# RWKV-7 recurrence slot: rank products, gates and decay sums one pair of heads ahead, head sums as 64-row products

## What is computed

```python
w_log = -softplus(-(w0 + tanh(xw @ w1) @ w2)) - 0.5
decay = exp(-exp(w_log))
a = sigmoid(a0 + (xa @ a1) @ a2)
kk = heads(k * k_k)
kk = kk / maximum(sqrt(sum(kk * kk, axis=-1)), 1e-12)
k = k * (1.0 + (a - 1.0) * k_a)
def step(S, inp):      # scan over the tokens, per head
    sa = einsum('bhvk,bhk->bhv', S, -kk_t)
    S = S * w_t + sa[..., None] * (kk_t * a_t) + v_t[..., None] * k_t
    return S, einsum('bhvk,bhk->bhv', S, r_t)
mean, var = y.mean(-1), y.var(-1)          # per head
y = (y - mean) * rsqrt(var + eps) * ln_w + ln_b
y = y + sum(rh * kh * r_k, axis=-1) * vh   # the bonus
out = (y * silu(z)) @ w_o
```

## Time and profile before

| | us |
|---|---|
| runs (3) | 2902.17, 2904.07, 2904.54 |
| median | 2904.07 |
| the profiled execution | 2901.24 |
| its span, first to last instruction | 2899.5 |
| PE busy | 2794.3 (96%) |
| DVE busy | 1337.7 (46%) |
| ACT busy | 1135.9 (39%) |

### The profile page before, as it was taken

How to read it: one execution, slowest core, us unless ns; L and a number is a source line. 1 busy time by engine, 2 the same in 40 slices (tenths; PEclk the granted TensorE clock), 3 DMA queues, 4 the chain that set the end, 5 groups by cost and what they waited for, 6 DMA issues and landing times.

```text
span 2899.5 us, 81414 instructions
## 1 busy us (share of the span) xinstructions
PE 2794.3 (96%) x37076; PEld 2632.0 (91%) x37076; DVE 1337.7 (46%) x2213; ACT 1135.9 (39%) x1559; POOL 108.1 (4%) x92
## 2 busy tenths in 40 slices
PE   6999999999999999999889899999999999999997
PEld 5899999999997888887789889999999999999997
DVE  7334313323327887787632364344443334444324
ACT  5344323324315555555432343343333343334322
POOL 0000000000001111111000000000000000000000
PEclk8999999999999999999999999999999999999999
DMA  3333333333311111112132242223222223222323
GB/s 124 110 104 110 111 111 111 112 111 141 104 67 47 53 53 53 53 53 78 31 130 88 81 143 75 96 75 98 89 89 75 97 75 97 90 89 75 125 89 108
DMA packets 79637, 262.25 MB, mean 90 GB/s; under 512 B 15936, under 2 KB 25920, under 8 KB 58816
## 3 DMA queue, kind: packets, MB, share of 16 engines
q1 hardware_dynamic: 70080, 239.23, 24.6%
q10 hardware_dynamic: 9216, 17.83, 1.6%
HBM read 216.06 MB, written 40.97 MB: 89 GB/s over the span
## 4 chain that ended last, share of the span: by engine, by line
PE 48%; ACT 1%; DVE 1%; issue 0%; DVEq 0%; ACTq 0%
PE t_pair L129 40%; PE t_lev L1596 1%; PE t_tok L1659 1%; PE t_pair L139 1%; PE t_lev L1670 1%; PE t_tok L1677 1%; PE t_tok L1637 0%; PE t_lev L1647 0%; PE t_tok L1552 0%; PE t_lev L1649 0%; PE t_lev L1609 0%; PE t_tok L1620 0%; PE t_tok L1629 0%; DVE keep_o L2179 0%; PE t_lev L1604 0%
## 5 line engine op out<-in xcount | busy, mean ns | idle before, releaser
L129 PE MATMUL t_pair<-t_x_hi,keep_w_hi 128*128 128x272 f32 x3008 | 660.1, 301 | 17.3 <-DVE t_x_lo L1992 9.1
L129 PE MATMUL t_pair<-t_x_lo,keep_w_hi 128*128 128x272 f32 x3008 | 623.8, 288 | 0.0
L129 PE MATMUL t_pair<-t_x_hi,keep_w_lo 128*128 128x272 f32 x3008 | 623.2, 288 | 0.0
L129 PEld LDWEIGHTS t_pair<-t_x_hi,keep_w_hi 128*128 128x128 f32 x3008 | 469.9, 189 | 48.5 <-issue 26.6
L129 PEld LDWEIGHTS t_pair<-t_x_lo,keep_w_hi 128*128 128x128 f32 x3008 | 475.6, 189 | 0.0
L129 PEld LDWEIGHTS t_pair<-t_x_hi,keep_w_lo 128*128 128x128 f32 x3008 | 472.4, 188 | 0.0
L129 PE MATMUL w_pair<-a_x_hi,keep_w_hi 128*128 128x272 f32 x2016 | 428.5, 294 | 19.4 <-DVE a_x_lo L1045 18.5
L129 PE MATMUL w_pair<-a_x_lo,keep_w_hi 128*128 128x272 f32 x2016 | 419.5, 289 | 0.0
L129 PE MATMUL w_pair<-a_x_hi,keep_w_lo 128*128 128x272 f32 x2016 | 417.4, 288 | 0.0
L1031 DVE TENSOR_TENSOR keep_w_lo<-keep_raw,keep_w_hi 128x2048 fp32r<-128x2048 f32 x63 | 144.4, 2293 | 469.7 <-ACT keep_w_hi L784 469.7
L129 PEld LDWEIGHTS w_pair<-a_x_hi,keep_w_hi 128*128 128x128 f32 x2016 | 320.3, 189 | 25.8 <-issue 20.7
(11 more groups left out here) (359 smaller groups left out, 3785.9 us busy)
## 6 DMA issues: line engine op xcount, KB each, us to landing
keep_raw<-in_w_in SPq DMA_DIRECT2D x64, 1024.0 KB, 4.9
keep_raw<-in_hgrn_in SPq DMA_DIRECT2D x64, 1024.0 KB, 4.9
keep_raw<-in_rwkv_wo SPq DMA_DIRECT2D x16, 1024.0 KB, 4.9
keep_raw<-in_hgrn_wo SPq DMA_DIRECT2D x16, 1024.0 KB, 4.9
t_Ss<-in_hgrn_s SPq DMA_DIRECT2D x16, 512.0 KB, 4.4
out_hgrn_s<-t_Sd SPq DMA_DIRECT2D x16, 512.0 KB, 6.7
scr_r<-a_stage ACTq DMA_DIRECT2D x16, 272.0 KB, 2.2
scr_k<-a_stage ACTq DMA_DIRECT2D x16, 272.0 KB, 2.1
```

Of the source, the lines that this page charges most:

```text
L129: mm = pe.matmul(out[:, a, 0:TH], w, x[:, kt, a * TH:(a + 1) * TH], start=(kt == 0 and n == 0), stop=(kt == KT - 1 and n == 2))
```

## The change

It rewrites the lists of PE, ACT and DVE for the slots; SyncE's and POOL's stay as they are.

- mean, variance, bonus (from pair 1) and square_sum (from pair 2) call by_heads: for each half of the columns two products of 64 rows, one per head, in place of one of 128 rows.
- rank_w(h) moves from behind level_yt(4) to ahead of level_x(3), and the rank_a of the pair ahead, h, from the start of the next slot to ahead of level_x(4). gate_w, gate_a, decay_sum and sum_before follow: they are made for h in slot i. Only decay_before(j) stays at the slot's start.
- g_and_value_y moves ahead of the third sample step. sample_states is cut in two: sample_values ahead of strict, the rest behind chain(i, 1).
- u_y is one group, all of chain(i, c) lie between levels 1 and 4, and variance moves from ahead of level_x(4) to behind inclusive, ahead of level_x(5).
- On DVE the three y steps come behind mask_x(j, 5), as the last of the slot.

```diff
@@ -415,6 +415,13 @@
                     mm = pe.matmul(q[:, a, 0:TH], lhsT, rhs[:, a * TH:(a + 1) * TH], start=True, stop=True)
                 return mm
 
+            def by_heads(lhsT, rhs):
+                for a in range(2):
+                    for hh in range(2):
+                        mm = pe.matmul(q[rows(hh), a, 0:TH], lhsT[rows(hh), rows(hh)],
+                                       rhs[rows(hh), a * TH:(a + 1) * TH], start=True, stop=True)
+                return mm
+
             def quarter(out, o_half, lhsT, rhs, i_half, start=True, stop=True):
                 return pe.matmul(out[rows(o_half)], lhsT[rows(i_half)], rhs[rows(i_half)], start=start, stop=stop,
                                  skip_group_check=not (start and stop))
@@ -444,8 +451,6 @@
             def rank_w(h):
                 pe.wait_ge(s.w2w_in, 16 * (h + 1))
                 pe.wait_ge(s.ssm, h + 1)
-                if h >= 2:
-                    pe.wait_ge(s.lnv, h - 1)
                 over_halves(w2[:, 0, :], lora[0]).then_inc(s.lora_w, 1)
 
             def rank_a(j):
@@ -457,12 +462,15 @@
                 pe.wait_ge(s.ksq, h + 1)
                 if h >= 1:
                     pe.wait_ge(s.bv, h)
-                over_halves(k.bones[:, :], ksq).then_inc(s.ss_mm, 1)
+                (by_heads if h >= 2 else over_halves)(k.bones, ksq).then_inc(s.ss_mm, 1)
 
             def bonus(j):
-                pe.wait_ge(s.sga, j + 1)
+                if j < 2:
+                    pe.wait_ge(s.sga, j + 1)
+                else:
+                    pe.wait_ge(s.lnv, j - 1)
                 pe.wait_ge(s.rk, j + 1)
-                over_halves(k.bones[:, :], rk).then_inc(s.bonus_mm, 1)
+                (by_heads if j >= 1 else over_halves)(k.bones, rk).then_inc(s.bonus_mm, 1)
 
             def strict(j):
                 a, b = at[j % 2], bt
@@ -539,10 +547,12 @@
                     pe.wait_ge(s.sU, 3 * i + n)
                 stacked(cut(m_ps, 0), cut(Ms, 0), Rs if n == 0 else Us[(n - 1) % 2]).then_inc(s.sMU_mm, 1)
 
-            def sample_states(i):
+            def sample_values(i):
                 pe.wait_ge(s.sU, 3 * i + 3)
                 pe.wait_ge(s.Vm, i + 1)
                 stacked(m_ps, cut(toks, 1), Vm[:, :, :].rearrange("p b v -> p (b v)"), True, False)
+
+            def sample_states(i):
                 pe.wait_ge(s.Um, i + 1)
                 stacked(m_ps, cut(toks, 0), Um[:, :, :].rearrange("p b v -> p (b v)"), False, True
                         ).then_inc(s.sd_mm, 1)
@@ -603,13 +613,13 @@
                 pe.wait_ge(s.y_ev, i + 1)
                 pe.wait_ge(s.sy, i + 1)
                 pe.wait_ge(s.bv, min(i + 2, KT))
-                pe.wait_ge(s.ssm, min(i + 3, KT))
-                over_halves(k.center[:, :], ybuf).then_inc(s.mean_mm, 1)
+                pe.wait_ge(s.sga, min(i + 3, KT))
+                by_heads(k.center, ybuf).then_inc(s.mean_mm, 1)
 
             def variance(i):
                 pe.wait_ge(s.ysq, i + 1)
                 pe.wait_ge(s.yc, i + 1)
-                over_halves(k.bones[:, :], ysq).then_inc(s.var_mm, 1)
+                by_heads(k.bones, ysq).then_inc(s.var_mm, 1)
 
             def first_pair(n, kt):
                 if (n, kt) == (51, 2):
@@ -691,74 +701,74 @@
             for i in range(KT):
                 j, h = i + 1, i + 2
                 back, front, ahead = i >= 0, 0 <= j < KT, h < KT
-                if front and i:
-                    rank_a(j)
                 if back:
                     sample_step(i, 0)
                     first_right(i)
                     sample_step(i, 1)
+                    g_and_value_y(i)
                     sample_step(i, 2)
-                    g_and_value_y(i)
                     u_and_value_state(i)
                 if front:
                     bonus(j)
                 if back:
                     rho_rest(i)
                     u_state(i)
+                    sample_values(i)
+                if front:
+                    strict(j)
+                if back:
+                    chain(i, 1)
                     sample_states(i)
-                    chain(i, 1)
-                if front:
-                    strict(j)
+                if front:
+                    level_x(j, 1)
                 if back:
                     chain(i, 2)
                 if ahead:
                     square_sum(h)
+                if front:
+                    level_yt(j, 1)
                 if back:
                     chain(i, 3)
                     sample_y(i)
                 if front:
-                    level_x(j, 1)
-                if back:
-                    u_y(range(4, NCH))
-                    state_y(i, 3)
+                    b_and_k_by_token(j)
+                    level_x(j, 2)
+                if back:
                     chain(i, 4)
-                    state_y(i, 2)
-                    state_y(i, 1)
-                if front:
-                    level_yt(j, 1)
-                    b_and_k_by_token(j)
+                    u_y(range(0, NCH))
+                if front:
+                    level_yt(j, 2)
                 if back:
                     chain(i, 5)
-                if front:
-                    level_x(j, 2)
-                if back:
-                    u_y(range(0, 4))
+                    for c in range(1, 4):
+                        state_y(i, c)
+                if ahead:
+                    rank_w(h)
+                if front:
+                    level_x(j, 3)
+                if back:
                     chain(i, 6)
                     state_y(i, 4)
+                    state_y(i, 5)
+                if front:
+                    a_and_v_by_token(j)
+                    level_yt(j, 3)
+                if back:
+                    chain(i, 7)
                     state_y(i, 6)
-                if front:
-                    level_yt(j, 2)
-                if back:
-                    state_y(i, 7)
-                    state_y(i, 5).then_inc(s.y_mm, 1)
-                if front:
-                    a_and_v_by_token(j)
-                    level_x(j, 3)
+                    state_y(i, 7).then_inc(s.y_mm, 1)
+                if ahead:
+                    rank_a(h)
+                if front:
+                    level_x(j, 4)
+                    samples(j)
                 if back:
                     mean(i)
                 if front:
-                    level_yt(j, 3)
-                    samples(j)
+                    level_yt(j, 4)
+                    inclusive(j)
                 if back:
                     variance(i)
-                if front:
-                    level_x(j, 4)
-                    inclusive(j)
-                    level_yt(j, 4)
-                if ahead:
-                    rank_w(h)
-                if back:
-                    chain(i, 7)
                 if front:
                     level_x(j, 5)
                     sample_right(j)
@@ -926,7 +936,7 @@
                 j, h = i + 1, i + 2
                 back, front, ahead = i >= 0, 0 <= j < KT, h < KT
                 if front and i:
-                    gate_w(j)
+                    decay_before(j)
                 if i == KT - 1:
                     act.wait_ge(s.o_in, 32)
                     for b in range(2):
@@ -934,13 +944,13 @@
                 if back:
                     act.wait_ge(s.sR_mm, i + 1)
                     act.copy(Rs[:, :], cut(m_ps, 0)).then_inc(s.sR, 1)
-                if front:
+                if front and i == 0:
                     gate_a(j)
                 if back:
                     act.wait_ge(s.r0ta_mm, i + 1)
                     act.copy(TA[:, C:], c1_ps[:, C:]).then_inc(s.ta, 1)
                     act.copy(R0[:, :], c0_ps[:, :]).then_inc(s.r0, 1)
-                if front:
+                if front and i == 0:
                     decay_before(j)
                 if back:
                     act.wait_ge(s.u0_mm, i + 1)
@@ -949,18 +959,24 @@
                     key_square(h)
                 if front:
                     decay_after(j)
+                if ahead:
+                    key_root(h)
                 if back:
                     act.wait_ge(s.sy_mm, i + 1)
                     act.copy(ybuf[:, SEQ:T], m_ps[:, 0:SMP]).then_inc(s.sy, 1)
+                if front:
+                    b_and_k_tokens(j)
                 if ahead:
-                    key_root(h)
-                if front:
-                    b_and_k_tokens(j)
+                    gate_w(h)
+                if front:
+                    a_and_v_tokens(j)
                 if back:
                     act.wait_ge(s.y_mm, i + 1)
                     act.copy(ybuf[:, 0:SEQ], y_ps[:, :]).then_inc(s.y_ev, 1)
-                if front:
-                    a_and_v_tokens(j)
+                if ahead:
+                    gate_a(h)
+                if front:
+                    sample_tokens(j)
                 if back:
                     act.wait_ge(s.mean_mm, i + 1)
```

(81 more changed lines are left out.)

10 lines of the change are left out of this document (2 added, 8 removed).

## The result

The changed kernel takes **2942.0 us**, median of 4 runs (2940.24 to 2947.89), against 2903.12 (2899.30 to 2904.54) for the kernel before: a ratio of 1.014, interval 1.0125 to 1.0155. The change makes the kernel 1.4% slower, 38.9 us between the medians. The forecast was 2949, its range 2927 to 2967. The profiled execution is the slowest of the four, 2947.89, with a span of 2946.1.

What follows compares the result with a forecast made beforehand. PE's own queue, with its waits, was taken to bound the kernel. Order 33 us, last slot's head sums -0.3 and clock 12 made 45 us more than 2904: 2949 us, 1.5% slower, range 2927 to 2967.

Steps and rivals of the forecast that it cites:

- The end of the slot: From variance to the next first_right (F): a serial ACT and DVE chain makes it 6.75 us, PE idle for 2.4.
- F to level_x(j,1): From first_right's start (F) to level_x(j,1): DVE's chain decides; 11.9 us, 1.1 shorter, with new PE waits of 1.0 and 1.2.
- The head sums: mean, variance, bonus, square_sum: eight 64-row records take 0.91 us instead of 1.12, about 0.3 saved each with the gap.
- Four times 0.3 is 1.3 us a slot: All four head sums in a slot were taken to save alike, 1.3 us a slot together.
- rival (d): Faster, 2868 us: head sums' 1.3 and b_Ti waits' 1.1 us kept, if variance to F takes only PE's 4.3; chance 0.05.
- level_x(j,1) to variance: Middle of the slot: 13.35 us becomes 20.25 as products move in, b_Ti waits go and two head sums save.
- The sum of the order: Whole slot: 11.9 + 20.25 + 6.75 = 38.9 us against 36.69, 2.2 a slot, 33 us over 15 slots.
- The clock: After PE's idle 2.4 us at a slot's end the clock may fall to 0.50, losing some 1.7 us each time.
- I take half, 12 us: Clock loss over the 15 slot ends, bounds 0 and 26 us; half taken since the sample step splits the gap.
- Rival (a): Same waits, but the clock stays at 2.4 GHz: 2904 + 33 = 2937 us; chance 0.2.
- (b): Clock also falls at the waits ahead of strict and level_x(1): up to 15 x 1.7 more, about 2972 us; chance 0.1.
- (c): By the bank rule each head sum takes 1.83 us, not 0.91: some 3 us a slot, about 2994; chance 0.03.

Runs made afterwards that it cites:

- experiment 4: Changed kernel with variance one product earlier, ahead of inclusive: 2932.94 us, ratio 1.0121 to the kernel before.
- experiment 7: Changed kernel with yz, the last DVE y step, moved behind the next slot's c_Mrk: 2925.13 us, ratio 1.0087 to the kernel before.
- experiment 5: Changed kernel with 16 extra pairs of constant products on PE behind level_yt(j,5), results unread: 2922.51 us, ratio 1.0083 to the kernel before.
- experiment 9: Changed kernel, third sample step ahead of g_and_value_y, yz behind next c_Mrk, Rs copy ahead of decay_before, 12 constant pairs in PE's closing gap: 2916.34 us, ratio 1.0051.
- experiment 1: Kernel before with all four head sums as 64-row products, old order kept: 2892.65 us against 2898.45, ratio 0.9977.
- experiment 2: Kernel before with only mean and variance as 64-row products, old order kept: 2890.26 us against 2901.99, ratio 0.9961.
- experiment 8: Changed kernel, third sample step ahead of g_and_value_y, yz behind next c_Mrk, ACT's Rs copy ahead of decay_before: 2921.13 us, ratio 1.0073 to the kernel before.

## Why the prediction was right, and where not

**The end of the slot: right.** variance to F was said to become 6.75, with PE idle for 2.4; it is 6.92, with 1.06 + 1.52 idle. Experiments 4 and 7 show the chain from both ends: PE work added inside costs nothing, and without yz on DVE the piece is 0.76 shorter. The Trainium skill (ScalarE: Activation LUTs, "Table sets") has exp and ln in one set; every trace here has a load of 1.28 us ahead of each. The Exp's is in the chain, the Ln's stands beside variance.

**F to level_x(j,1): right.** Said: strict at 8.7, then 3.2. Measured at full clock: 8.66 and 3.19. So is the cause: from DVE's sample_u(i,2) to strict it is 5.58 us in each slot 1 to 12 of experiment 5, and the third sample step behind g_and_value_y costs 0.55 (8.66 against 8.11 in experiment 9). The waits of PE stand where they were said to, 1.06 us for b_Ti of level 1 where 1.2 was said, but only 0.5 for c_S where 1.0 was said. PE's own work ahead of strict was added up wrongly too, as its terms make 7.4 and not 7.7; PE also waits for c_TA (8.9 us in 15 waits) and once in a while for b_rk. As DVE decides, none of this reached the sum.

**The head sums: price right, place wrong.** Eight records in 0.92, said 0.91. The step "Four times 0.3 is 1.3 us a slot" failed for the old order: two of the four lie ahead of products that wait for another engine, and 0.55 is left (experiments 1 and 2). In the new order bonus was priced inside a wait and so at nothing, and the gain there is 0.89 clean (38.93 to 38.04), most of it the 0.78 that was said for mean and square_sum. It didn't harm the sum, but rival (d), which kept all 1.3, was built on it. The rule on row tiles and banks (the Trainium skill, TensorEngine Tiling, "Restrictions and Gotchas") is contradicted by the rows of 64x272 as it was by the state products: one by one the eight records would take 1.83 us by the prediction's estimate.

**level_x(j,1) to variance: over-priced.** Said 20.25, clean 19.27. The rank products, said 1.27 each, take 1.14 and 1.26, which is 0.14 of the miss. The traces divide most of the rest (slot 10 before, slot 8 of experiment 5, from start to next start). The pauses ahead of level_x(2) and level_x(3) took 0.65 and 0.53 us in the old order, not the 0.86 of idle time that was taken off, since the record ahead of a pause is still shown as busy in it: 0.32. The four small products ahead of level_x(j,1) took 2.86 before and take 2.25 now; 0.4 is the head sum's, and the other 0.2 was time that PE had there while first_inverse ran. Some 0.2 are short gaps ahead of 128-row products, one counted twice (ahead of rank_w), one gone with variance. About 0.1 stays open.

**The sum of the order: 2.2 a slot said, 1.7 measured.** The clean pieces make 38.04, said 38.9: the step that was mis-sized is the piece above. Against the mean slot of before, 36.55, the kernel with its clock held up (experiment 5) has 38.30: 1.75 a slot, 25 us in 15 slots by the profile and 24 by the ratio, where 33 were said.

**The clock: right in kind, wrong in size.** "I take half, 12 us" failed: it fell at every one of the 15 ends in the profiled execution, and gave 16.5 us when it was kept up. The price of a fall was said to be 1.7; it is 16.5 / 15 = 1.1 by the times, and 1.4 by the profiles (F to strict 10.07 against 8.66). Only what is slow ahead of DVE's sample_u(i,2) is paid: that start moves from F + 3.07 to between + 3.77 and + 4.86, while from there to strict it stays 5.58 us in 11 of 12 slots. The slow work behind it is stretched into the wait for DVE. The sample step of 0.33 between the two gaps didn't protect the clock, which was the reason for taking half.

**Sum.** 33 - 0.3 + 12 = 45 us said; 24 + 16.5 = 40.5 measured, which is the ratio of 1.014 (38.9 between the medians). The two errors, 9 too much and 4.5 too little, partly cancel; that the time was closer than its terms is luck. Rival (a), at 2937 without the clock, is refuted by experiment 5 although its number is near; (b) has no support: the waits ahead of strict and level_x(1) leave no stretch of 0.50 in slots 1 to 12 once the end is filled. (c) falls with the rule. (d) fell on the place it named.

## What to carry to other kernels

Moving work into small waits pays only if the work isn't what covered a longer chain elsewhere: before an instruction is moved, look at what runs on the other engines behind the place it leaves, and add that chain up. Each saving on the busy engine needs its next wait named: here more than half of the head sums' gain went into waits that were there already, and a small part of the change (two sums, in the old order) is the kernel to keep, 0.4% faster than before. A gap on PE can cost more than its length, when the clock falls behind it; if it can't be closed, work of no use in it may be worth more than nothing. And a wait that looks like waste can take up pauses from elsewhere, as the one ahead of strict did.

## What the runs showed of the hardware

**The clock fell more readily than the old kernel let expect.** In the earlier trace rows PE had been busy for 1.24 of 3.41 us. Here two gaps of 1.06 and 1.52 us with 0.33 of work between were enough in each of 15 slots. With 1.9 us of products in the first gap (experiment 5) it didn't fall at the ends of slots 0 to 13. With one gap 0.76 shorter (experiment 7) it fell at 7 ends of 15, and with one gap of 1.86 us (experiment 8) at 12. At the ends of the kernel after it stayed at 0.50 for 3.4 to 6.8 us.

**The "issue" pauses keep time with instruction fetches.** In the kernel before, all 10 such pauses of PE between 880 and 1430 us end 2.3 to 2.8 us after a fetch of 16 KB on the queue of instructions begins. The longest, 2.38 us, ends at 1363.87; its fetch begins at 1361.50, and the view of DMA by queue, 1361 to 1362 us, has it (queue and kind, packets, MB, share):

```profile
q8 instruction: 1, 0.02, 6.0%
```

The 24 of experiment 9 end 2.3 to 3.0 us after one. There are 124 fetches of this size in that stretch of the kernel before, and most are followed by no pause. That is an agreement in time and nothing more: no run changed the fetches. Whether they cause the pauses, and why experiment 9 has more of them, stays open. Neither of its two edits brings them alone: experiment 5, with filler, has 11 (6.0 us) in the same stretch besides those at F, and experiment 8, with the repairs, 13 (6.4 us).
